# Even attention: the value products of two heads interleaved on the two column halves, and eight chunks of modulation sums placed after the attention

## The reference

```python
k_c, v_c = mla_kv(ckv_a, ck_pe, kv_norm, w_kvb, None)
k_l, v_l = mla_kv(kv_a, k_pe, kv_norm, w_kvb, rope)
q_l = mla_q(q_a, q_norm, w_qb, rope)
a_l = dense_attention(q_l, concat([k_c, k_l]), concat([v_c, v_l]), MLA_SCALE)   # softmax(q k) v
y_l = concat([fourier_mix(f_in) * silu(f_gate), a_l * silu(m_gate)]) @ w_out
...
mod = silu(c) @ w_mod[l] + b_mod[l]        # shift, scale and gate rows; the same for block two with w_ada
x = x + gate * y
```

## Time and profile before

| | |
|---|---|
| median of three runs | 1455.68 us |
| the profiled execution's own time | 1452.23 us |
| its span | 1450.4 us |
| granted TensorE clock, mean | 0.967 of full |
| TensorE busy | 1355.8 us (93%) |
| DVE busy | 951.8 us (66%) |
| ACT busy | 496.6 us (34%) |
| GpSimd busy | 144.3 us (10%) |
| all L1859 sums into `modulation_sums` | 148.6 us in 112 operations |

### The profile page before, as it was taken

One profiled execution on the slowest core, in us unless ns is written; L12 is line 12 of the kernel. 1 busy time (PEld: TensorE's weight loads), 2 busy tenths in 40 slices (PEclk: granted clock), 3 DMA queues, 4 the chain that ended last, 5 costly groups with the idle time before them and its releaser, 6 DMA issues.

```text
span 1450.4 us, 18938 instructions
## 1 busy us (share of the span) xinstructions
PE 1355.8 (93%) x7889; PEld 1100.2 (76%) x7889; DVE 951.8 (66%) x1227; ACT 496.6 (34%) x742; POOL 144.3 (10%) x163
## 2 busy tenths in 40 slices
PE   5999999999988899999998999997999999899996
PEld 1589756546775449888986989884988898799894
DVE  3577477766558675676778666666665768755546
ACT  1422025403245323533232443423354232343331
POOL 2010110100000010012321000001000222100000
PEclk9999999999999999999998999998999999999998
DMA  9453350334330256574774676644665676355551
GB/s 347 145 176 117 110 201 29 117 116 147 123 119 35 92 189 235 189 262 165 280 267 149 232 268 226 200 166 150 210 210 201 223 299 213 121 177 200 175 191 42
DMA packets 104918, 257.97 MB, mean 178 GB/s; under 512 B 8217, under 2 KB 11770, under 8 KB 104578
## 3 DMA queue, kind: packets, MB, share of 16 engines
q1 hardware_dynamic: 80554, 171.78, 34.7%
q0 software_dynamic: 20192, 75.58, 14.3%
q10 hardware_dynamic: 4088, 9.41, 1.9%
HBM read 255.70 MB, written 1.05 MB: 177 GB/s over the span
## 4 chain that ended last, share of the span: by engine, by line
PE 76%; DVE 13%; ACT 4%; DMA 3%; issue 3%; POOL 1%; ACTq 0%; SPq 0%; POOLq 0%; DVEq 0%
PE bank L743 73%; PE bank L890 3%; DVE weights_low L2041 2%; DMA weight_ring<-in_w_in_dram 2%; ACT weights_high L1458 1%; DMA x<-in_ctx_dram 1%; ACT odd_prob L1632 1%; POOL inverse_roots L654 1%; DVE statistics L2001 1%; DVE statistics L1899 1%; DVE x L2473 1%; DVE x L2000 0%; DVE odd_weights_low L2041 0%; DVE xn L1994 0%; DVE statistics L2023 0%
## 5 line engine op out<-in xcount | busy, mean ns | idle before, releaser
L2041 DVE TENSOR_TENSOR weights_low<-weight_ring,weights_high 128x2048 fp32r<-128x2048 f32 (+1 forms) x124 | 276.9, 2234 | 270.1 <-ACT weights_high L1458 270.0
L1458 ACT ACTIVATE weights_high<-weight_ring 128x2048 fp32r<-128x2048 f32 (+1 forms) x124 | 231.2, 1865 | 444.4 <-PE bank L743 362.6
L743 PE MATMUL bank<-uT_high,weights_high 128*128 128x256 f32 (+1 forms) x1200 | 345.0, 288 | 7.5 <-DVE uT_low L2318 3.6
L743 PE MATMUL bank<-uT_low,weights_high 128*128 128x256 f32 (+1 forms) x1200 | 343.0, 286 | 0.0
L743 PE MATMUL bank<-uT_high,weights_low 128*128 128x256 f32 (+1 forms) x1200 | 342.8, 286 | 0.0
L743 PEld LDWEIGHTS bank<-uT_high,weights_high 128*128 128x128 f32 (+1 forms) x1200 | 232.1, 193 | 13.4 <-ACT gate_tanh L1771 6.1
L743 PEld LDWEIGHTS bank<-uT_low,weights_high 128*128 128x128 f32 (+1 forms) x1200 | 232.1, 193 | 1.0
L743 PEld LDWEIGHTS bank<-uT_high,weights_low 128*128 128x128 f32 (+1 forms) x1200 | 232.0, 193 | 0.5
L1859 DVE SCALAR_TENSOR_TENSOR modulation_sums<-modulation_ring,silu_c_columns,modulation_sums 128x1024 f32<-128x1024 f32 x112 | 148.6, 1327 | 18.3 <-DMA modulation_ring<-in_w_ada_dram 10.0
L743 PE MATMUL bank<-weights_high,hidden_high 128*128 128x512 f32 x256 | 102.9, 402 | 4.4 <-DVE weights_low L2041 4.4
L743 PE MATMUL bank<-weights_low,hidden_high 128*128 128x512 f32 x256 | 102.4, 400 | 0.0
(11 more groups left out here) (297 smaller groups left out, 2208.1 us busy)
## 6 DMA issues: line engine op xcount, KB each, us to landing
weight_ring<-in_w_in_dram SPq DMA_DIRECT2D x52, 1024.0 KB, 6.7
modulation_ring<-in_w_ada_dram POOLq DMA_DIRECT2D x48, 1024.0 KB, 7.2
weight_ring<-in_w_up_dram SPq DMA_DIRECT2D x32, 1024.0 KB, 5.4
weight_ring<-in_w_down_dram SPq DMA_DIRECT2D x32, 1024.0 KB, 5.0
modulation_ring<-in_w_mod_dram POOLq DMA_DIRECT2D x16, 1024.0 KB, 5.4
weight_ring<-in_o_w_in_dram SPq DMA_DIRECT2D x10, 1024.0 KB, 5.2
weight_ring<-in_w_branch_dram SPq DMA_DIRECT2D x16, 512.0 KB, 3.8
weight_ring<-in_w_o_dram SPq DMA_DIRECT2D x8, 1024.0 KB, 7.1
```

Source lines behind the costliest of these rows:

```text
L743: return track(pe.matmul(*args, **kw))
L1458: act.activation(ring[:, s, 0:kn * cols], wring[:, slot, 0:kn * cols], ACT.Copy).then_inc(S["high_ready"], 1)
L2041: dve.tensor_tensor(lo[:, s, 0:kn * cols], wring[:, slot, 0:kn * cols], hi[:, s, 0:kn * cols].bitcast(F32), ALU.subtract).then_inc(w_free[ ...
```

## The change

The value products of heads 2g and 2g+1 are done together, in step 2g+3 rather than one in step 2g+2 and one in 2g+3, and alternate between the two column halves matmul by matmul. They stand ahead of the transposes in their step. `reduce_part(4, 1)` moves ahead of the last value products. On DVE the product with the gate (now L2155) moves ahead of the copy of part 2 of the transposes. The four chunks of row 5 leave the attention and stand after the rotary operations, `gemv(6, 0)` follows them, and chunks 1 to 3 of row 6 each follow one `half_out` of `eout0`. GpSimd's and SyncE's lists are unchanged.

```diff
--- before.py
+++ after.py
@@ -1025,8 +1025,29 @@
                         ins = product(o[:, N * i:N * i + N], qT_e[:, h, N + P * i:N + P * i + P],
                                         kT_e[:, h, N:2 * N], start=True, stop=True)
                     done(ins, ("S", h, 2))
-                if h == MH:
-                    reduce_part(4, 0)
+                if h >= MH:
+                    reduce_part(4, h - MH)
+                if h >= 3 and h % 2 == 1:
+                    g = (h - 3) // 2
+                    pv = start(("PV", g))
+                    for i in range(2):
+                        for j in range(2):
+                            copied(("PT", 2 * g + j, i))
+                    for kb in range(TALL):
+                        for j in range(2):
+                            r, a = HD * j, 2 * g + j
+                            product(pv[r:r + HD, 0:N], ev[:, kb, NOPE * a:NOPE * a + NOPE],
+                                    probT_e[:, j, kb // 2, N * (kb % 2):N * (kb % 2) + N],
+                                    start=(kb == 0), stop=(kb == 3), skip_group_check=True)
+                    for j in range(2):
+                        copied(("PT", 2 * g + j, 2))
+                    for kb in range(TC):
+                        for j in range(2):
+                            r, a = HD * j, 2 * g + j
+                            ins = product(pv[r:r + HD, N:2 * N], ev[:, TC + kb, NOPE * a:NOPE * a + NOPE],
+                                          probT_e[:, j, 2, N * kb:N * kb + N], start=(kb == 0), stop=(kb == 1),
+                                          skip_group_check=True)
+                    done(ins, ("PV", g))
                 if 1 <= h <= MH:
                     a = h - 1
                     pe.wait_ge(S["p_ready"], a + 1)
@@ -1037,24 +1058,6 @@
                                 c = COLS * q + P * (2 * i + j) if i < 2 else 2 * COLS + N * q + P * j
                                 ins = turn(o[:, N * j + P * q:N * j + P * q + P], prob_e[:, a % 2, c:c + P], P)
                         done(ins, ("PT", a, i))
-                if h >= 2:
-                    a = h - 2
-                    r = HD * (a % 2)
-                    if a % 2 == 0:
-                        pv = start(("PV", a // 2))
-                    copied(("PT", a, 0))
-                    copied(("PT", a, 1))
-                    for kb in range(TALL):
-                        ins = product(pv[r:r + HD, 0:N], ev[:, kb, NOPE * a:NOPE * a + NOPE],
-                                        probT_e[:, a % 2, kb // 2, N * (kb % 2):N * (kb % 2) + N],
-                                        start=(kb == 0), stop=(kb == 3))
-                    copied(("PT", a, 2))
-                    for j in range(2):
-                        ins = product(pv[r:r + HD, N:2 * N], ev[:, TC + j, NOPE * a:NOPE * a + NOPE],
-                                        probT_e[:, a % 2, 2, N * j:N * j + N], start=(j == 0), stop=(j == 1))
-                    if a % 2 == 1:
-                        done(ins, ("PV", a // 2))
-            reduce_part(4, 1)
             for g in range(4):
                 copied(("f2", g))
                 copied(("PV", g))
@@ -1578,14 +1581,13 @@
                         if i != 2:
 
                             release(ins, job)
-                if h == MH:
-                    gate_rows(4, grow_e)
+                if h >= MH:
+                    gate_rows(4, grow_e, parts=(h - MH,))
                 if 1 <= h <= MH:
                     a = h - 1
                     for i in range(2):
                         o = ready(("PT", a, i))
                         copy_out(("PT", a, i), probT_e[:, a % 2, i, :], o[:, :])
-            gate_rows(4, grow_e, parts=(1,))
 
 
 
@@ -2143,23 +2145,21 @@
                         maxima(ready(("S", h, i))[:, :], h, i).then_inc(S["max_ready"], 1)
                     dve.tensor_reduce(negmax[:, b, 2:4], ready(("S", h, 2))[:, :].rearrange("p (i n) -> p i n", i=2),
                                       AX_X, ALU.max, negate=True).then_inc(S["max_ready"], 1)
-                    if h >= 4:
-                        gemv(5, h - 4)
                     copied(("S", h, 2))
                     link(dve.reciprocal(rsum[:, b, :], esum[:, b, :]))
                     normalise([prob_e[:, b, 0:COLS], prob_e[:, b, COLS:2 * COLS],
                                prob_e[:, b, 2 * COLS:2 * COLS + N], prob_e[:, b, 2 * COLS + N:3 * COLS]], h)
-                if 1 <= h <= MH:
-                    a = h - 1
-                    o = ready(("PT", a, 2))
-                    ins = dve.tensor_copy(probT_e[:, a % 2, 2, :], o[:, :])
-                    release(ins, ("PT", a, 2))
                 if h >= 3 and h % 2 == 1:
                     g = (h - 3) // 2
                     o = ready(("PV", g))
                     ins = dve.scalar_tensor_tensor(out=eyT[:, 4 + g, :], in0=o[:, :], scalar=0.5,
                                                    in1=eyT[:, 4 + g, :], op0=ALU.mult, op1=ALU.mult)
                     release(ins, ("PV", g))
+                if 1 <= h <= MH:
+                    a = h - 1
+                    o = ready(("PT", a, 2))
+                    ins = dve.tensor_copy(probT_e[:, a % 2, 2, :], o[:, :])
+                    release(ins, ("PT", a, 2))
 
             dve.wait_ge(pos_in, 16)
             link(dve.tensor_copy(posf[:, :], posi[:, :]))
@@ -2180,11 +2180,14 @@
             dve.tensor_scalar(rotary[:, 3, :], rotary[:, 3, :], -1.0, 1.5707963267948966, ALU.mult, ALU.add
                               ).then_inc(S["angles_ready"], 1)
             for q in range(4):
-                gemv(6, q)
+                gemv(5, q)
+            gemv(6, 0)
             for v in range(2):
                 copied(("mod", 4, v, 1))
             for i in range(TALL):
                 link(half_out(("eout", 0, i), i, 0, grow_e[i // TC], etmp[:, i % 2, :]))
+                if i > 0:
+                    gemv(6, i)
 
             def normal_o(i):
 
```

## The result

Over 20 runs each the changed kernel takes 1456.14 us (1451.05 to 1461.29), the kernel before 1450.01 us (1445.29 to 1455.94). The ratio is 1.0035, interval 1.0022 to 1.0048: slower by about 5 us. The change costs time although the attention it speeds up gets 8.8 us shorter.

A forecast was written before the change was run, and what follows sets the result against it. TensorE was taken to set the attention's pace. The terms -8.2 + 10.8 + 2.4 gave +5.0 us, added to 1455.68 us, the median of the runs shown: 1460.7 us, own range 1456 to 1464, 8 in 10 for 1451 to 1468.

The forecast's parts named there:

- The attention: Even attention: alternating value products take 2.81 us a pair instead of 5.46, so `eout0` starts 8.2 us earlier.
- The sums behind it: Between `eout0` and `eout1`: moved sums delay the last `half_out`; TensorE stands 11.8 us, the 8.2 and 2.6 us are lost.
- The bias row behind (6,1): Ahead of `gemv(6, 0)`: its bias row, queued behind chunk (6,1), lands with that chunk at 301.3 us.
- DVE's order: Beside `eout0`: row 6 chunks of 2.6 us between `half_out` of 2.18 us put the last one at 315.6 us.
- The landing of (6,1): Load beside SyncE's slab: chunk (6,1), issued at 293.8, usable at 301.3 us, between 300.1 and 303.1.
- The clock: Start of `eout1` after TensorE's pause: a granted clock of 0.50 costs 2.4 us, bounds 0 and 3.1.
- within: Whole kernel: the change ends within about 0.5% (7.3 us) of no change; chance 0.63.
- the sums don't hold up `eout1`: Rival ahead of `eout1`: the last `half_out` is ready behind TensorE, the 8.2 us remain, 1447.5 us; chance 0.08.
- the halves don't overlap here: Rival in the even attention: two heads still take 13.66 us, `eout1` restarts about 14 us late, 1472 us; chance 0.04.
- the longer stall: Rival ahead of `eout1`: chunk (6,1) and its bias land later, for instance 303.5; +8 to +12, 1466 us; chance 0.22.
- the short one: Rival ahead of `eout1`: the slab doesn't disturb, the clock comes up at once; +1 us, 1457, inside the forecast's range.

The follow-up runs named there:

- the second profile: The changed kernel run again unaltered, beside the kernel before; ratio to before 1.0031.
- The filler: The changed kernel with twelve matmuls, their result overwritten unread, added ahead of `eout1`; ratio to the kernel before 1.0021.
- the sums alone: The kernel before with only the sums of rows 5 and 6 moved as in the change, attention matmuls as before; ratio to before 1.0074.
- head by head: The changed kernel with a pair's twelve value products at the same place, one head after the other instead of alternating; ratio to the kernel before 1.0060.
- bias row first: The changed kernel with row 6's clearing and bias row ahead of the loads of chunks (6,0) and (6,1) in GpSimd's list; ratio to the kernel before 1.0000.

## Why the prediction was right or wrong

**The attention: right.** Predicted 8.2 us gained, measured 8.76. The products take 2.74 us a pair (2.81 predicted from the odd attention), and the pace of 11.08 us for two heads is that of DVE's loop. A pair without overlap would have stayed at 5.46 us, which no profile shows. The rule of the Trainium skill ("TensorE: Matmul & The Clock Gate", "Part 3: Packing small matmuls") that only loads to other row groups overlap, which I had read as leaving a pair at 5.46 us, does not hold for these column halves: the trace has 2.74 us.

**The sums behind it: right in mechanism, and closer in size than the steps deserve.** From `eout0` to the start of `gemv(6, 0)` 24.3 us were predicted and 299.41 - 275.13 = 24.28 measured; from `eout0` to `eout1` 39.5 predicted and 39.68 measured. The bias row behind (6,1) is confirmed by moving it, DVE's order by exchanging it. The landing of (6,1), the most open term, was 8.5 us after its issue; I had 301.3 - 293.8 = 7.5. It was issued 290.64 - 275.13 = 15.5 us behind `eout0` and not 16.8, because DVE began its sums 1.6 us behind `eout0` and not 2.1, and the loads of (5,2) and (5,3) landed in 5.3 and 5.4 us and not in 5.7 and 6.3. That the two errors cancel to 0.02 us is luck.

**The clock: right in kind, a little too dear.** 2.4 us were taken, 15.71 - 13.97 = 1.74 measured, 1.97 in the second profile. What the price follows is not the pause's length but how long the low clock lasts into `eout1`: 3.5 us here, half of which is the loss. The filler shows the pause as the cause.

**The sum.** Predicted were -8.2 + 10.8 + 2.4 = +5.0 us. Measured in the profile are -8.76 for the attention, 39.68 - 28.76 = +10.92 from `eout0` to `eout1`, and +1.74 for the clock: +3.90. The ratio says +5.1, or +4.5 in the second set, and the stages +3.84 and +4.06; what lies between that and +5.1 is inside the interval and was not settled.

**What was wrong** is the step from this sum to the chances: "a measurement of this kernel tells about 0.5% (7.3 us) from no change", and so "within" as the likeliest case at 0.63. I had sized that from three runs 6.6 us apart, and no row showed it. With 20 runs each side the interval is 0.13% either way, a sum of +5.0 us is 0.34%, and the outcome is a slowdown clear of the noise. The working said slower, and the headline said no change. The same three runs spoiled the level: their median of 1455.68 stands 5.7 us above the 1450.01 of 20 runs, so the forecast of 1460.7 was 4.6 us above the measured 1456.14 though the difference was about right. Against 1450.01 it reads as +10.7 us, about twice what came. To add the sum to the profiled execution (1457.2) would have been nearer.

**The rivals.** That the sums don't hold up `eout1` is refuted by the sums alone; that the halves don't overlap here by the 2.74 us. Neither the longer stall nor the short one came: the pause is 11.98 us where 11.8 were predicted.

## What to carry to other kernels

Work moved out of a loop to make room lands ahead of something else on its engine: follow the engine's list to the next operation that frees a buffer for the bound engine, and put the moved work behind that one. Loads that were hidden because they ran beside a long stage become a chain when their consumers move together behind it, and a small row queued behind a large one can be as late as the large one (here 6.7 us instead of 2.2). Judge a change of some microseconds by stage in the traces and by many runs in total; the total of two profiles had the wrong sign here.

## What the runs showed of the hardware

- A pair of 64-column matmuls on the two column halves starts within 0.01 us and costs the time of one. The overlap is not tied to strict alternation: head by head, eight of the twelve pairs that 24 records could form still start together, which is why a group takes 3.73 us where a lone head's pace (12 records in 2.73 us) would give 5.46.
- The clock's price did not follow the length of the pause. Pauses of 6.54, 6.54, 10.28, 11.64, 11.67 and 11.98 us cost 2.44, 2.79, 1.71, 2.20, 1.97 and 1.74 us in the 32 records behind them; a pause of 1.67 us behind filler work cost nothing. In the same order the granted clock stayed at 0.50 for 4.9, 5.6, 3.4, 4.4, 4.0 and 3.5 us after `eout1` had begun, and the price is half of that each time.
- Three loads of a megabyte that meet stretch each other: in the changed kernel the first, chunk (6,0), took 5.5 us to land, SyncE's slab behind it 9.5 us and chunk (6,1) 8.5 us, where two chunks that met took 5.3 and 5.4 us there and 5.6 and 6.2 us before. No run takes one of the three away, so that the others are the reason is not shown.
- A row of 4 KB issued behind a megabyte on the same queue landed with it: the bias row of row 6 took 6.7 us behind chunk (6,1) and landed within 0.2 us of it, 3.6 us behind chunk (5,3) in "bias row first", and 2.2 us in the kernel before, where none of the queue's chunks was under way.
